# Cross attention of a hybrid block on the raw residual: transposes inside the output projection, key products by head, value products by head pair

## The chip, the cores and the metric

One core of a Trainium2 chip runs one launch that computes one layer of a hybrid encoder block, all in float32, for 512 tokens of width 1024. The metric is the device time of the launch in microseconds. Five compute engines are named as in the profile: PE (matmuls and transposes), ACT (copies, squares, exponentials), DVE (vector work that reads PSUM or SBUF), POOL (SBUF only) and SP (it issues most DMAs). Each runs its own instructions in order.

## The reference, cut to what matters

```python
h = rmsnorm(x, g_mix);  x = x + parallel_mixers(h, ...)        # ends in merged @ w_out
h = rmsnorm(x, g_x);    m = rmsnorm(mem, g_mem)                 # x: 512 x 1024, mem: 256 x 1024
q = (h @ w_cq)          # 512 x (4 heads x 128)
k = (m @ w_ck);  v = (m @ w_cv)                                 # 256 x (4 x 128)
p = softmax(q k^T * 128 ** -0.5, axis=-1)                       # per head, 512 x 256
x = x + (p v) @ w_co
h = rmsnorm(x, g_ffn);  x = x + hierarchical_moe(h, ...)        # 4 groups, top 1; 8 experts in it, top 2
out = rmsnorm(x, g_final)
rmsnorm(x, g) = x * rsqrt(mean(x * x) + 1e-6) * g
```

Since the root of a token is one factor for its whole row, q and the scores of a token can carry it or leave it out until the softmax. The 32 experts have 3 MB of weights each (gate and up 1024 x 256, down 256 x 1024).

## The kernel before

`job_order()` writes one list of jobs for PE, by hand; every other engine walks the same list in the same order and does its part of each job. A job is a tuple. Its product goes to one of eight PSUM banks, given out in turn (`bank_index`, L295 to L312); a job waits until the job that had the bank before it is emptied (`before_in_bank`), by ACT or by DVE (`emptied_by`), unless that one is in `PARTIAL`, whose sums are left standing for a later job. `emptied` counts jobs in the order of the list, so a job of DVE counts as emptied only when DVE has finished all that stands ahead of it. `wo` jobs sit in the bank of their `wp`.

The residual `xres` is four tiles of 128 tokens (t = 0 to 3). Products that need more than one pass of fp32r are split: `h_hi` and `w_high` are rounded copies (ACT), `h_lo` and `w_low` the remainders (DVE, POOL), and `split_sums` adds hi*hi, hi*lo and lo*hi (L1032 to L1034), so one 128 x 512 product over K of 128 is three matmuls. Weights come through a ring of three 1 MB chunks. ACT makes the high part of a chunk (`high_part`) and POOL its low part (`low_part`, L839), at the job named in `split_at`; SP loads the next chunk when the low part is made, or for unsplit weights when their last job is done.

The jobs around the change, in order:

- `wp`, `wo` (n, t): the two halves of K of the output projection, columns 512 n, tile t, 12 matmuls each. DVE adds the sum to `xres` (L1949).
- `hT x` (t, q): four PE transposes of tile t, half q of its columns, into one bank; DVE scales by the norm's gains into `hT` (L1794), ACT makes `h_hi` (`high_of_hT`), DVE `h_lo` of the first half (`low_of_hT`, L1748) and POOL of the second (L845). Before them, ACT squares each row (L1603), DVE takes the roots for two tiles at a time (`rms`), and ACT scales the rows (`scaled_rows`, L1472) into two buffers.
- `ck` (hp): the keys of a pair of heads from `memT`; `cq` (h): the queries of head h, 24 matmuls; ACT copies them to `cqT`.
- `xs` (t, hp): scores of tile t and head pair hp. DVE takes the negated maximum (L1972), ACT the exponentials and their sums (L1621), DVE the reciprocals (L1976), POOL scales the probabilities (L904).
- `xp` (t, hp): four transposes of the probabilities; ACT copies them to `probT[t % 2]`.
- `xv` (t): the value product of all four heads, a bank each tile. ACT makes its high part in `h_hi`, DVE its low part (L1959), which empties it.
- `co` (t, n): the projection of the heads, 12 matmuls; DVE adds it to `xres` (L1980), ACT squares (L1640).
- `hT ffn`, `rt`, `pos` (t): transposes for the router, router logits, slots. In `rt` DVE runs a chain of some fifteen small operations (L1989 to L1758). `ra`, `g0`, `ls`, `most` end the list.

SP's queue, in its own order: chunks; expert 0's weights behind the first cq chunk, when `merged_ready` is full; expert 1's when the last ck is done; parts of 3 when cq(3) is done; expert 5's (in the ring) when the last chunk's low part is made; one part of 2 after the last `xs`, one after xv(3), the last and one of 3 after co(3,1); expert 4's after the last normed row; then each expert's buffer is refilled as soon as the expert six before it has left it (L792, L794).

## Time and profile before

| what | us |
|---|---|
| median of 3 runs | 861.79 (860.40 to 869.06) |
| profiled execution, its own time | 860.8 |
| its span | 859.0 |
| PE busy | 787.2 (92%) |
| DVE, ACT, POOL busy | 358.4, 242.3, 289.3 |
| DMA, mean over the span | 189 GB/s |

The span is the profiled part of one execution; the execution's own time is 1.8 us longer. Busy shares are means over stages: PE is busy nearly throughout, the DMA engines are full only in the last third, where the experts' weights come in.

### The profile page before, as it was taken

To read this page: it belongs to the slowest core of one execution; us is meant where nothing else is said; L and a number is where in the kernel's file an instruction comes from. 1 tells how busy PE (TensorE), PEld (TensorE's weight loads), DVE (VectorE), ACT (ScalarE), POOL (GpSimd) and SP (SyncE) were. 2 spreads that over 40 slices of the span, in tenths; PEclk is the share of its full clock that TensorE was granted. 3 is DMA by queue.
4 is the path that set the end of the run, shared out by engine and by line. 5 is a ranking of instruction groups with operands and counts; after the bars stand their busy time and mean duration, and the time that the engine had idled before them with its cause. 6 is when DMAs were issued, how large, how long until landed. Compare 5 with 4: busy or idle time off the path is not lost. (4 is left out here: it accounts for less than half of the span.)

```text
span 859.0 us, 14860 instructions
## 1 busy us (share of the span) xinstructions
PE 787.2 (92%) x5803; PEld 639.6 (74%) x5803; DVE 358.4 (42%) x757; ACT 242.3 (28%) x421; POOL 289.3 (34%) x255
## 2 busy tenths in 40 slices
PE   5999999899899999999999898998999999887884
PEld 4888888788788877788887777886777777665651
DVE  6479752473574683336612712363222222211115
ACT  4332342112212559422214444331111111100102
POOL 3824434442242244043350634233333333322110
PEclk9999999999999999999999899999999999999997
DMA  9754423402202250455476273659999999999946
GB/s 258 144 103 91 103 45 66 83 1 50 50 1 50 50 142 11 94 142 153 98 146 196 54 241 116 252 219 343 391 389 388 388 383 390 384 383 391 390 157 243
DMA packets 73230, 162.77 MB, mean 189 GB/s; under 512 B 18834, under 2 KB 46306, under 8 KB 65240
## 3 DMA queue, kind: packets, MB, share of 16 engines
q1 hardware_dynamic: 65712, 150.66, 55.6%
q0 software_dynamic: 5472, 9.82, 3.4%
q10 hardware_dynamic: 1992, 1.55, 0.9%
q8 instruction: 36, 0.59, 0.3%
q14 instruction: 18, 0.15, 0.1%
HBM read 157.31 MB, written 13.04 MB: 198 GB/s over the span
## 5 line engine op out<-in xcount | busy, mean ns | idle before, releaser
L1032 PE MATMUL bank<-h_hi,w_high 128*128 128x512 f32 x296 | 122.4, 414 | 2.3 <-DVEq L560 2.0
L839 POOL TENSOR_TENSOR ring_low<-ring,w_high 128x2048 fp32r<-128x2048 f32 (+1 forms) x16 | 71.3, 4459 | 135.1 <-ACT w_high L1448 118.4
L1033 PE MATMUL bank<-h_lo,w_high 128*128 128x512 f32 x296 | 115.8, 391 | 0.0
L1373 PEld LDWEIGHTS bank<-arena,hT 128*64 128x64 f32 x1728 | 96.8, 136 | 24.9 <-issue 24.5
L1373 PE MATMUL bank<-arena,hT 128*64 128x128 f32 x1728 | 100.6, 274 | 8.8 <-DMA arena<-in_w_exp_up 7.9
L839 POOL TENSOR_TENSOR w_low<-ring,w_high 128x2048 fp32r<-128x2048 f32 x14 | 64.4, 4598 | 81.7 <-ACT w_high L1448 81.6
L2043 DVE SCALAR_TENSOR_TENSOR rt<-rt,bank 128x128 f32<-128x128 f32 x32 | 9.2, 288 | 176.9 <-ACT rt L1664 176.9
L1448 ACT ACTIVATE w_high<-ring 128x2048 fp32r<-128x2048 f32 (+1 forms) x32 | 58.8, 1838 | 47.1 <-PE bank L1034 30.9
L1032 PEld LDWEIGHTS bank<-h_hi,w_high 128*128 128x128 f32 x296 | 55.8, 188 | 14.8 <-DVEq L560 2.3
L1034 PE MATMUL bank<-h_hi,ring_low 128*128 128x512 f32 x168 | 66.1, 394 | 0.0
L1033 PEld LDWEIGHTS bank<-h_lo,w_high 128*128 128x128 f32 x296 | 55.8, 188 | 9.5
L1383 PE MATMUL bank<-arena,rt 128*64 128x512 f32 x216 | 52.3, 605 | 10.4 <-DVE rt L2047 10.4
L956 POOL DMA_INDIRECT y_half<-rows,cst x32 | 32.6, 1019 | 79.4 <-ACT rows L1668 78.6
L1032 PE MATMUL bank<-w_high,h_hi 128*128 128x512 f32 (+1 forms) x144 | 51.7, 359 | 1.5 <-ACT w_high L1448 1.5
L1034 PE MATMUL bank<-w_high,h_lo 128*128 128x512 f32 (+1 forms) x144 | 51.0, 354 | 0.0
L1034 PE MATMUL bank<-h_hi,w_low 128*128 128x512 f32 x128 | 50.0, 390 | 0.0
L1668 ACT ACTIVATE rows<-bank 128x512 f32<-128x512 f32 x32 | 19.1, 598 | 109.3 <-PE bank L1383 109.3
L1033 PE MATMUL bank<-w_low,h_hi 128*128 128x512 f32 (+1 forms) x128 | 44.7, 349 | 0.0
L1664 ACT ACTIVATE rt<-bank 128x128 f32<-128x128 f32 x32 | 8.9, 278 | 109.2 <-PE bank L1373 109.2
L951 POOL DMA_INDIRECT hT<-h_rows,rt x31 | 30.4, 981 | 24.5 <-POOL rt L946 23.8
L1448 ACT ACTIVATE arena<-bank 128x512 f32<-128x512 f32 (+1 forms) x39 | 23.3, 597 | 53.7 <-PE bank L1034 35.6
L1034 PEld LDWEIGHTS bank<-h_hi,ring_low 128*128 128x128 f32 x168 | 31.5, 188 | 7.4
(309 smaller groups left out, 1412.0 us busy)
## 6 DMA issues: line engine op xcount, KB each, us to landing
arena<-in_w_exp_gate SPq DMA_DIRECT2D x27, 1024.0 KB
arena<-in_w_exp_up SPq DMA_DIRECT2D x27, 1024.0 KB
arena<-in_w_exp_down SPq DMA_DIRECT2D x27, 1024.0 KB
ring<-in_w_in SPq DMA_DIRECT2D x33, 512.0 KB, 6.7
ring<-in_w_exp_gate SPq DMA_DIRECT2D x5, 1024.0 KB
ring<-in_w_exp_up SPq DMA_DIRECT2D x5, 1024.0 KB
ring<-in_w_exp_down SPq DMA_DIRECT2D x5, 1024.0 KB
xres<-in_x SPq DMA_DIRECT2D x8, 512.0 KB, 7.0
```

Source lines behind the costliest of these rows:

```text
L839: after(pool.tensor_tensor(low, full, high, ALU.subtract), w_lo)
L951: pool.indirect_dma_start(out=xg[:, b % DEEP, :], out_offset=None, in_=h_rows, in_offset=bass.IndirectOffsetOnAxis(ap=idx[b][0:CAP, :], ax ...
L956: pool.indirect_dma_start(out=y_half, out_offset=bass.IndirectOffsetOnAxis(ap=at_y, axis=0), in_=ysb[:, y, :], in_offset=None, bounds_chec ...
L1032: pe.matmul(o, l_hi, r_hi, start=(n == 0), stop=False)
L1033: pe.matmul(o, l_hi, r_lo, start=False, stop=False)
L1034: ins = pe.matmul(o, l_lo, r_hi, start=False, stop=(n == count - 1))
L1373: ins = pe.matmul(bank[CAP * half:CAP * half + CAP, 1, P * n:P * n + P], xgT[:, x, kk, :], w[:, kk, P * half:P * half + P], start=(kk == 0 ...
L1383: ins = pe.matmul(bank[CAP * half:CAP * half + CAP, o, :], hidT[:, CAP * kk:CAP * kk + CAP], down[:, kk, 512 * half:512 * half + 512], sta ...
L1448: after(nc.scalar.activation(o, i, ACT.Copy, scale=scale), s)
L1664: nc.scalar.activation(gate_th, bank[:, 1, 0:P], ACT.Tanh, scale=0.5).then_inc(gth_ready, 1)
L1668: nc.scalar.activation(ysb[:, y, :], bank[:, 4 + b % 2, :], ACT.Copy).then_inc(y_sb, 1)
L2043: nc.vector.scalar_tensor_tensor(out=gated, in0=gate_th, scalar=1.0, in1=bank[:, 1, 0:P], op0=ALU.add, op1=ALU.mult).then_inc(step["dve"], 1)
```

## The change

The transposes for the cross attention read `xres` itself. Those of the first half of the columns (q = 0) stand among the jobs of the second half of the output projection, those of the second half behind each tile's `wo`. The queries and scores are then those of the raw residual times the gains; the root comes in as the scale of the exponential and as a factor on the maximum (one DVE operation more per `xs`). `scaled_rows` and the two-tile roots of this phase go; the squares are taken into `rows`, and one four-tile root is taken by DVE behind the last low part. `ck` is split by head, the second pair's behind cq(1). `xw` (t) is the value product of heads 0 and 1, left standing in its bank, `xv` (t) that of heads 2 and 3 in the same bank. For tiles 2 and 3 (`t >= X_POOL`) DVE makes both halves of the low part. ACT makes the high part of the last co chunk at xs(0,1) and no longer at xv(0). SP waits for `ck` (1,1) where it waited for `ck` (1), and since chunks go by first use, the first cq chunk now comes ahead of the second ck chunk. The diff, with little of what stands around it:

```diff
@@ -166,17 +166,17 @@
         jobs += [(k, f) for k in ("ub", "ua") for f in range(4 * half, 4 * half + 4)]
-    jobs += [(k, n, t) for n in range(2) for k in ("wp", "wo") for t in range(NT)]
-    turn = [[("hT", "x", t, q) for q in range(2)] for t in range(NT)]
-    jobs += turn[0] + turn[1] + [("ck", 0)] + turn[2] + turn[3] + [("ck", 1)]
-
-    for hp in range(2):
-        jobs += [("cq", 2 * hp)] + [("xp", t, 0) for t in range(2)] * hp + [("cq", 2 * hp + 1)] + [("xs", t, hp) for t in range(NT)]
-    jobs += [("xp", 0, 1), ("xp", 1, 1)]
-    tail = [("xv", 0), ("xp", 2), ("xv", 1), ("co", 0), ("xp", 3), ("xv", 2), ("T", 0), ("co", 1), ("rt", 0),
-            ("xv", 3), ("T", 1), ("co", 2), ("rt", 1), ("pos", 0), ("T", 2)]
+    jobs += [(k, 0, t) for k in ("wp", "wo") for t in range(NT)]
+    turn = [[("hT", "x", t, q) for t in range(NT)] for q in range(2)]
+    jobs += [("wp", 1, 0), ("wp", 1, 1), turn[0][0], ("wp", 1, 2), turn[0][1], ("wp", 1, 3), turn[0][2]]
+    jobs += [("wo", 1, 0), turn[0][3], ("wo", 1, 1), turn[1][0], ("wo", 1, 2), turn[1][1], ("wo", 1, 3), turn[1][2]]
+    jobs += [("ck", 0, 0), turn[1][3], ("ck", 0, 1), ("cq", 0), ("cq", 1), ("ck", 1, 0), ("ck", 1, 1)] + [("xs", t, 0) for t in range(NT)]
+    jobs += [("cq", 2), ("cq", 3), ("xp", 0, 0), ("xp", 1, 0), ("xs", 0, 1), ("xs", 1, 1), ("xs", 2, 1), ("xw", 0), ("xw", 1)]
+    jobs += [("xp", 0, 1), ("xs", 3, 1), ("xp", 1, 1), ("xp", 2, 0)]
+    jobs += [("xv", 0), ("xp", 3, 0), ("xv", 1), ("xw", 2), ("xp", 2, 1), ("co", 0, 0), ("co", 0, 1), ("xp", 3, 1)]
+    tail = [("xv", 2), ("xw", 3), ("T", 0), ("co", 1), ("rt", 0), ("xv", 3), ("T", 1), ("co", 2), ("rt", 1), ("pos", 0), ("T", 2)]
     for stage, t in tail:
-        if stage in ("xv", "rt", "pos"):
+        if stage in ("xv", "xw", "rt", "pos"):
@@ -187,7 +187,7 @@
-PARTIAL = ("gp", "wp", "g0", "ra")
+PARTIAL = ("gp", "wp", "g0", "ra", "xw")
@@ -195,6 +195,7 @@
 LAST_TILE = NT - 1
+X_POOL = 2
@@ -288,6 +289,7 @@
         split_at[said.get(c) or first_use[split_chunks[m - 1]]] = m
+    high_at = {("xs", 0, 1) if job == ("xv", 0) else job: m for job, m in split_at.items()}
@@ -299,6 +301,8 @@
             bank_index[job] = bank_index["wp", job[1], job[2]]
+        elif job[0] == "xv":
+            bank_index[job] = bank_index["xw", job[1]]
@@ -759,7 +763,7 @@
                 if n == place[("co", 0)]:
-                    job_done(sp, ("ck", 1))
+                    job_done(sp, ("ck", 1, 1))
@@ -868,7 +872,7 @@
                     after(pool.tensor_scalar(gain_b, gain_b, 0.5, None, ALU.mult))
-                if job[:2] == ("hT", "x") and c == 1:
+                if job[:2] == ("hT", "x") and c == 1 and job[2] < X_POOL:
@@ -1066,8 +1070,8 @@
                     _, phase, t, q = job
-                    if phase == "ffn":
-                        job_empty(pe, ("co", t, q))
+                    if phase in ("ffn", "x"):
+                        job_empty(pe, ("co", t, q) if phase == "ffn" else ("wo", q, t))
@@ -1076,11 +1080,9 @@
                         return ins
-                    else:
-                        pe.wait_ge(rows_ready, NORM_TILES[phase] - NT + t + 1)
+                    pe.wait_ge(rows_ready, t + 1)
                     for j in range(4):
-                        source = mem_rows[:, t] if phase == "mem" else rows[:, t % 2]
-                        ins = pe.transpose(oh4[:, j], source[:, (4 * q + j) * P:(4 * q + j + 1) * P], ident)
+                        ins = pe.transpose(oh4[:, j], mem_rows[:, t, (4 * q + j) * P:(4 * q + j + 1) * P], ident)
@@ -1253,9 +1255,8 @@
                     job_empty(pe, ("hT", "mem", NM - 1, 1))
-                    for i in range(2):
-                        ins = sums(o[:, MEM * i:MEM * i + MEM], [(wide(chunks_of(job)[0])[:, kk, P * i:P * i + P], memT[:, kk, :]) for kk in range(KD)])
-                    return ins
+                    i = job[2]
+                    return sums(o[:, 0:MEM], [(wide(c0)[:, kk, P * i:P * i + P], memT[:, kk, :]) for kk in range(KD)])
@@ -1264,13 +1265,13 @@
                     pe.wait_ge(h_hi_ready["x"], 2 * NT)
-                    pe.wait_ge(h_lo_ready["x"], NT)
-                    pe.wait_ge(pool_lo_ready["x"], NT)
+                    pe.wait_ge(h_lo_ready["x"], 2 * NT - X_POOL)
+                    pe.wait_ge(pool_lo_ready["x"], X_POOL)
                     job_empty(pe, ("cq", 2 * hp + 1))
-                    job_empty(pe, ("ck", hp))
+                    job_empty(pe, ("ck", hp, 1))
@@ -1282,10 +1283,10 @@
                     return ins
-                if k == "xv":
-                    t = job[1]
-                    job_empty(pe, ("xp", t, 1))
-                    for h in range(X_HEADS):
+                if k in ("xw", "xv"):
+                    t, hp = job[1], int(k == "xv")
+                    job_empty(pe, ("xp", t, hp))
+                    for h in (2 * hp, 2 * hp + 1):
@@ -1458,18 +1459,11 @@
+                if phase == "x":
+                    job_done(act, ("wo", 1, t))
                     copy(h_hi[:, 4 * q:4 * q + 4, t * P:(t + 1) * P], hT[:, 4 * q:4 * q + 4, t * P:(t + 1) * P], h_hi_ready[phase])
-
-            def scaled_rows(phase, t, source):
-
-                base = NORM_TILES[phase]
-                act.wait_ge(rstd_ready, {"mem": 1, "x": 2 + t // 2}[phase])
-                if t >= 2:
-                    job_done(act, ("hT", phase, t - 2, 1))
-                dst = rows[:, t % 2, :] if phase != "mem" else source
-                after(nc.scalar.activation(dst, source, ACT.Copy, scale=rstd[:, base + t:base + t + 1]), rows_ready)
@@ -1489,16 +1483,23 @@
                     return
+                act.wait_ge(rstd_ready, 1)
                 for t in range(tiles):
-                    scaled_rows(phase, t, source(t))
+                    after(nc.scalar.activation(source(t), source(t), ACT.Copy, scale=rstd[:, base + t:base + t + 1]), rows_ready)
+
+            def x_square(t):
+
+                n = NORM_TILES["x"] + t
+                job_empty(act, ("wo", 1, t))
+                after(nc.scalar.activation(rows[:, t % 2, :], xres[:, t, :], ACT.Square, accum_out=squares[:, n:n + 1]), squared)
                 c = job[-1]
-                if job in split_at:
-                    high_part(split_at[job])
+                if job in high_at:
+                    high_part(high_at[job])
@@ -1596,34 +1597,29 @@
                 if k == "wo" and job[1] == 1:
-                    base = NORM_TILES["x"]
-                    if c == 2:
-                        scaled_rows("x", 0, xres[:, 0, :])
-                    job_empty(act, job)
-                    after(nc.scalar.activation(x_row[c], xres[:, c, :], ACT.Square, accum_out=squares[:, base + c:base + c + 1]), squared)
-                    if c == 2:
-                        scaled_rows("x", 1, xres[:, 1, :])
-                    for t in (2, 3) if c == 3 else ():
-                        scaled_rows("x", t, xres[:, t, :])
-                        high_of_hT("x", t - 2)
-                    for t in (2, 3) if c == 3 else ():
-                        high_of_hT("x", t)
+                    if c < 2:
+                        x_square(c)
+                if job[:2] == ("hT", "x") and c == 1:
+                    high_of_hT("x", job[2])
+                    for t in (2, 3) if job[2] == NT - 1 else ():
+                        x_square(t)
                     if t == 0 and hp == 0:
-                        act.wait_ge(h_lo_ready["x"], NT)
-                        act.wait_ge(pool_lo_ready["x"], NT)
+                        act.wait_ge(h_lo_ready["x"], 2 * NT - X_POOL)
+                        act.wait_ge(pool_lo_ready["x"], X_POOL)
                         h, so = 2 * hp + i, 16 * t
+                        n = NORM_TILES["x"] + t
                         ins = nc.scalar.activation(prob[t][:, h, :], o[:, MEM * i:MEM * i + MEM], ACT.Exp, bias=xstat[:, so + 4 + h:so + 5 + h],
-                                                   accum_out=xstat[:, so + 8 + h:so + 9 + h])
+                                                   scale=rstd[:, n:n + 1], accum_out=xstat[:, so + 8 + h:so + 9 + h])
                 if k == "xp":
-                    if job[1] >= 2 and c == 0:
-                        job_done(act, ("xv", job[1] - 2))
+                    if job[1] >= 2:
+                        job_done(act, ("xv" if c else "xw", job[1] - 2))
@@ -1746,6 +1742,10 @@
                 after(tt(h_lo[s], hT[s], h_hi[s].bitcast(F32), ALU.subtract), h_lo_ready[phase])
+                if phase == "x" and t >= X_POOL:
+                    dve.wait_ge(h_hi_ready[phase], 2 * t + 2)
+                    s = (slice(0, P), slice(4, KD), slice(t * P, (t + 1) * P))
+                    after(tt(h_lo[s], hT[s], h_hi[s].bitcast(F32), ALU.subtract), h_lo_ready[phase])
@@ -1778,8 +1778,6 @@
                         mark(ins) if h < 3 else after(ins, y_ready)
-                if job == ("wo", 1, 2):
-                    rms(NORM_TILES["x"], 2, rstd_ready)
@@ -1797,6 +1795,8 @@
                             low_of_hT(phase, t)
+                            if phase == "x":
+                                rms(NORM_TILES["x"], NT)
@@ -1947,8 +1947,6 @@
                     after(stt(out=xs, in0=o, scalar=0.5, in1=xs, op0=ALU.mult, op1=ALU.add), e)
-                    if (n, t) == (1, 3):
-                        rms(NORM_TILES["x"] + 2, 2, rstd_ready)
@@ -1960,7 +1958,7 @@
                 if k == "ck":
-                    after(nc.vector.tensor_copy(ckT[:, 2 * c:2 * c + 2, :], o.rearrange("p (h m) -> p h m", h=2)), e)
+                    after(nc.vector.tensor_copy(ckT[:, 2 * job[1] + c, :], o[:, 0:MEM]), e)
@@ -1969,7 +1967,9 @@
                     job_done(dve, job)
-                    after(nc.vector.tensor_reduce(xstat[:, 16 * t + 4 + 2 * hp:16 * t + 6 + 2 * hp], o.rearrange("p (h m) -> p h m", h=2), AX, ALU.max, negate=True), xmax_ready)
+                    least, n = xstat[:, 16 * t + 4 + 2 * hp:16 * t + 6 + 2 * hp], NORM_TILES["x"] + t
+                    after(nc.vector.tensor_reduce(least, o.rearrange("p (h m) -> p h m", h=2), AX, ALU.max, negate=True))
+                    after(ts(least, least, rstd[:, n:n + 1], None, ALU.mult), xmax_ready)
```

## Rows read from the trace of the kernel before

**Rows 1.** The page: span; TensorE's granted clock and the DMA share in 40 slices.
```profile
span 859.0 us, 14860 instructions
...
PEclk9999999999999999999999899999999999999997
...
DMA  9754423402202250455476273659999999999946
```

**Rows 2.** Chain that ended last, in order of time: start us, us, what.
```profile
624.59 17.37 DMA ring<-in_w_exp_up
```

**Rows 3.** Windows: length, busy of PE, PEld, DVE, ACT, POOL; granted clock, DMA share, GB/s.
```profile
558.00:568.00 10.00, 10.00 (x69) 9.09 (x69) 7.21 (x35) 5.97 (x9) 3.70 (x11) 1.00 0.13 54
...
573.00:583.00 10.00, 9.71 (x118) 9.45 (x118) 5.89 (x29) 0.92 (x1) 2.14 (x8) 1.00 1.00 400
```

**Rows 4.** Timeline of SP's DMA queue, expert weights: start us, us, what.
```profile
568.81 0.38 SPq L727 DMA_DIRECT2D arena<-in_w_exp_down  x1
...
585.89 0.36 SPq L792 DMA_DIRECT2D arena<-in_w_exp_gate  x1
```

**Rows 5.** Windows around the two falls of TensorE's clock, columns as in Rows 3.
```profile
466.00:470.00 4.00, 2.26 (x18) 1.95 (x18) 0.69 (x1) 3.90 (x5) 0.00 (x0) 1.00 0.07 27
...
477.00:484.00 7.00, 4.41 (x18) 3.98 (x19) 6.62 (x12) 5.13 (x7) 2.44 (x2) 0.64 0.71 153
...
522.00:526.00 4.00, 2.35 (x15) 1.67 (x13) 2.31 (x6) 3.77 (x15) 2.43 (x3) 1.00 0.88 365
...
526.00:532.00 6.00, 5.06 (x33) 4.85 (x32) 0.67 (x2) 4.74 (x7) 3.93 (x3) 0.72 0.00 0
```

**Rows 6.** Timeline of PE: start us, us, line, what, count, idle before and its releaser.
```profile
465.75 0.39 PE L1034 MATMUL bank<-w_high,h_lo 128*128 128x512 f32 x1
...
469.84 7.07 PE L1025 MATMUL bank<-arena,ring 128*128 128x256 f32 x32
...
479.01 1.92 PE L1083 MATMUL bank<-cst,rows 128*128 128x128 f32 x8 [2.09 <-ACT rows L1472]
...
483.24 8.37 PE L1025 MATMUL bank<-arena,ring 128*128 128x256 f32 x32
...
503.33 3.69 PE L1025 MATMUL bank<-arena 128*128 128x256 f32 x16 [0.79 <-issue]
...
527.21 3.46 PE L1025 MATMUL bank<-rows,arena 128*128 128x128 f32 x16 [0.94 <-ACT rows L1448]
```

**Rows 7.** Timelines of POOL (L839, L845) and DVE (L1717, L1748), columns as in Rows 6.
```profile
470.91 4.53 POOL L839 TENSOR_TENSOR w_low<-ring,w_high 128x2048 fp32r<-128x2048 f32 x1 [19.74 <-ACT w_high L1448]
...
480.33 1.27 POOL L845 TENSOR_TENSOR h_lo<-hT,h_hi 128x512 fp32r<-128x512 f32 x1 [4.89 <-ACT h_hi L1448]
...
472.03 3.43 DVE L1717 TENSOR_SCALAR tiny<-tiny 128x2 f32<-128x2 f32 x1 [5.09 <-ACT hT L1603]
...
480.56 1.58 DVE L1748 TENSOR_TENSOR h_lo<-hT,h_hi 128x512 fp32r<-128x512 f32 x1
```

**Rows 8.** Timelines of ACT and POOL in the second half of the cross attention.
```profile
521.69 0.47 ACT L1621 ACTIVATE hT<-bank,tiny 128x256 f32<-128x256 f32 x1 [2.11 <-PE bank L1025]
...
527.73 1.91 ACT L1448 ACTIVATE w_high<-ring 128x2048 fp32r<-128x2048 f32 x1
...
523.26 1.04 POOL L904 TENSOR_TENSOR hT<-hT,tiny 128x512 f32<-128x512 f32 x1 [6.39 <-DVE tiny L1976]
```

**Rows 9.** Timelines of PE (first three) and DVE about the first router tile.
```profile
549.34 2.03 PE L1025 MATMUL bank<-rows,arena 128*128 128x128 f32 x16
...
551.21 1.04 PE L1072 MATMUL bank<-cst,xres 128*128 128x128 f32 x8
...
552.00 0.48 PE L1032 MATMUL bank<-w_high,h_hi 128*128 128x512 f32 x1
...
549.65 0.22 DVE L1989 SCALAR_TENSOR_TENSOR rt<-bank,tiny,rt 128x4 f32<-128x4 f32 x1 [0.90 <-PE bank L1025]
...
553.04 0.69 DVE L1959 TENSOR_TENSOR h_lo<-bank,h_hi 128x512 fp32r<-128x512 f32 x1
```

## Prediction, on record before the changed kernel was run

> **What bounds the kernel now.** Read the page's slices first [rows 1]: from about 580 us on the DMA engines are full to the end, and the chain [rows 2] turns from PE to expert weights at 624.6 us and stays with them until 806. So the expert stage is a stream of fixed length, and only its start can move. What sets the start is in the windows and SP's queue: at 558 to 568 us the DMA engines are nearly empty (0.13), from 573 us they are full [rows 3]; the loads that fill them are issued when co(3,1) is done (568.8) and, from expert 6 on, when expert 0's gate and up products are done (585.9) [rows 4]. Both hang on PE. A microsecond that PE gains before them moves the whole stream, and the end, by one. So the question is when PE reaches the router; the experts and the tail only shift.
>
> Between the end of the output projection (the last of its matmuls starts at 465.75, 0.23 behind the one ahead, so it ends at 466.0 [rows 6]) and the router PE loses time in two ways. It idles: 1.7 us in 466 to 470 [rows 5], 2.09 and then 0.58 us before the transposes of tiles 2 and 3, 0.79 before the first scores [rows 6], 1.65 in 522 to 526 [rows 5], 0.94 before xv(0) [rows 6]. And its clock falls twice to the 1.2 GHz level, after the idle of 2.09 and after the idles of 522 to 527 (granted 0.64 and 0.72 in those windows [rows 5]). The first fall costs 3.1 us: eight transposes take 1.92 for 1.04 [rows 6, 9], twice, and ck(1) 8.37 for ck(0)'s 7.07 [rows 6]. The second costs 1.6: xv(0) takes 3.46 [rows 6], xv(3) 1.87 (549.34 to the next group, 551.21 [rows 9]).
>
> **The change, part by part.** I lay the new order out with durations of the rows: an output-projection job is 12 matmuls of 0.227, 2.72 us; four transposes 0.4 (0.79 for eight, 551.21 to 552.00 [rows 9]; I take 0.43, with the switch of bank); one head's key product half of 7.07, 3.54; a cq job 24 matmuls, 5.44; xs 0.86 (3.46 for four [rows 6]); an xw or xv, half of the old xv, 0.9. The number of matmuls stays.
>
> *To cq(0).* The old second half of the projection begins 8 x 2.72 ahead of 466.0, at 444.2. The new order puts 32 transposes and two key products with it: 21.8 + 8 x 0.43 + 7.1 = 32.3, so PE could begin cq(0) at 476.5. The two row scalings per pair of tiles, the rstd chain and PE's waits on them are gone: nothing waits for the norm before the exponentials (the four-tile root follows at 480 to 482 on DVE, 15 us before scores; cost nothing, hidden by cq and ck). The old cq(0) began after all of ck, at 491.3 (483.24 and 8.37, less the overlap [rows 6]); with the later two key products set off it would be 484.2. So the order is worth 7.7 here.
>
> *But the low parts are late.* ACT makes the high part of the cq weights after hi(1), at 467.9 to 469.8 (1.91 as in [rows 8]), and POOL then takes 4.53 for the low one [rows 7], 469.9 to 474.5. DVE comes to low(1), a subtraction of two SBUF operands, at 470.3. Such DVE work does not run beside POOL's: the 128x2 operation at 472.03 took 3.43 and ended with POOL's at 475.4, and a low part at 480.56 took 1.58, 0.7 behind POOL's end at 481.6 [rows 7]. So low(1) ends at 475.2, ck(0,0)'s copy and hT(3,1) at 476.3, and then come four subtractions of 0.72, since tiles 2 and 3 now have both halves on DVE: 479.2. cq(0) waits for the last: idle 2.8. Gain so far 7.7 - 2.8 = 4.9. The 0.4 us by which POOL is ahead of DVE decide this order; the other one is rival (e).
>
> *Scores.* ck(1,0) and ck(1,1) stand behind cq(1) and cover its copy: the 0.79 idle [rows 6], and 0.4 of overlap behind it, go. cq(3)'s copy is covered by xp(0,0) and xp(1,0), another 1.0. By xs(0,1) the gain is 7.1: 512.5 for 519.7. DVE's extra scaling of the maxima has no row; a small operation takes about 0.2 alone, and up to a whole product of POOL's (1.04 [rows 8]) if it blocks as the one at 472.03 did. I find it 0.4 late at three of eight, laid beside POOL's queue; in the first half that is behind cq(2) and costs nothing. ACT's exponentials take their scale from a column now: now 0.47 each [rows 8]; I take no more, and 0.1 on each would still stay behind PE's work in the first half.
>
> *xp to co(0,0).* ACT now does the high part of the last co chunk (1.91 [rows 8]) ahead of the exponentials of xs(0,1). Its queue: copies of cq(3), xp(0,0), xp(1,0) until 513.7, high part until 515.6, two pairs until 518.0; POOL's product follows one reciprocal later, 517.2 to 518.3 (1.04). PE is through xw(1) at 516.9: it waits 1.4 for xp(0,1), then 0.25 for xp(1,1), 0.7 for the copy behind xv(1), 0.3 and 0.8 for xv(0) and xv(1) to leave the banks that xp(2,1) and co(0,0) take. Those 3.5 stand against about 4.8 of old idling and slow clock there: gain 8.4 at co(0,0), equal work against equal work.
>
> *Two new bank waits.* The turn of banks shifts. co(1,0) comes into the bank of xv(2), and is behind ACT's square, xp(3,1)'s copy, xv(2)'s high part and DVE's low one: 1.3 of idle; 7.1 is left. co(2,0) comes into the bank of xv(3), which it did not before. DVE empties xv(3) only after the router chain of rt(0): 549.65 to 553.04, plus 0.69 [rows 9], so 4.4 behind the end of rt(0). PE needs only xv(3) at 0.9 and eight transposes, 1.8, before co(2,0). Idle 2.7. What is left at co(2,0) is 4.4 (547.6 for 552.0). From there PE runs as before. The same addition over the old order falls 0.3 short of its trace, so I take 4.1.
>
> *SP.* cq(0)'s chunk loads before expert 0's weights, cq(2)'s at 476.8, landing near 483, before ACT's use; the last co chunk lands behind 3 MB of expert 1 near 511.6, 2 us before ACT wants it. Costs nothing; if it came 1 us after 513.7, that microsecond would be PE's.
>
> *Clock.* The old order lost 4.7 to it, of which part lay in idles that it shortened; that is in the 4.1. The new one has two idles of 2.7 to 2.8, longer than the 2.09 behind the first fall [rows 6]; but 1.7 in 466 to 470 brought none [rows 5]. A fall with busy work behind costs what the second did, 1.6. None costs 0; both long ones (3.1 each) 6.2. I take one of 1.6: 4.1 - 1.6 = 2.5.
>
> **Sum.** 2.5 us off the profiled execution's 860.8 (span 859.0 and 1.8 around it) is 858.3. The median of the runs shown, 861.79, stands 1.0 above that execution, so a median would be **859.3**.
>
> **Rivals.** (a) *The clock never falls:* 4.1 gained, 857.7. For it: full-rate work for 30 us ahead of the stall. Against: 2.09 sufficed [rows 5, 6]. (b) *The new waits are not there:* DVE slips between POOL's, and the router chain is shorter than I read; then 4.1 + 2.8 + 2.7 = 9.6, 852.2. For it: only their absence removes the ground for both falls too. Against: both waits are in the order of the code, with rows for each length. (c) *Slower, the clock at cq(0) and co(2,0):* it falls at both idles and stays down through the next waits, as the first fall did; 2 x 3.1 = 6.2 against 4.1, so 863.9. It decides once more than 4.1 us is lost, that is 8 us at 1.2 GHz. Against: behind both stalls stand 10.9 and 5.4 us of matmuls without a wait, where the old fall had more waits. (d) *The start doesn't carry:* the stream begins when it did, 861.8. Against: the DMA engines are at 0.13 before it [rows 3]. (e) *DVE's low(1) gets in ahead of POOL:* POOL then runs 471.0 to 475.6, DVE does hT(3,1) under it, the four subtractions end at 478.5, the idle before cq(0) is 2.0 and the sum 0.8 larger, 858.5. For it: 0.4 us is little beside ACT's and POOL's own start times; against, the order as the rows' durations give it. The Trainium skill, "SBUF — State Buffer", section "Who interferes with whom", has a rule for this: of a GpSimd operation and a VectorE one with two SBUF inputs, the one that is issued first keeps the shared ports for the whole instruction and the other blocks.
>
> **Chances.** Forecast (one fall, or two short ones, 858.5 to 861) 0.36; (e) 0.14; (a) 0.17; (b) 0.15; (c) 0.13; (d) 0.05. The range 852.5 to 863.5 leaves out the faster part of (b) and most of (c). What can be told from no change here is 1%, 8.6 us: faster than 853.2 needs the larger part of (b), 0.11; slower than 870.4 has 0.02; within 0.87.
>
> **What would show it.** In the changed trace: no idle on PE among transposes and projection; DVE's L1748 for tile 1 stretched to the end of POOL's L839, PE idle 2 to 2.8 before cq(0); idle 2.7 before co(2,0), released by DVE's L1959 behind the router chain; granted clock under 1.0 near either. Expert 0 then starts 2 to 4 us ahead of 582. If the DMA engines show a gap in 590 to 800 us, or PE is still idle for other reasons before rt(0), the reading is wrong.

## The result, and the profile after

The changed kernel was **slower**: median 868.06 us (865.78 to 872.34, 17 runs) against 863.4 (860.3 to 871.55, 17 runs) for the kernel before in the same comparison; ratio 1.0061 [1.0039, 1.0082]. The profiled execution took 870.23 (span 868.4, mean granted clock 0.974). The loss of 0.6% is under the 1% that the forecast called no change, but outside its range of 852.5 to 863.5: all 17 runs of the changed kernel took 865.78 or more, 12 of the 17 of the kernel before less. The comparisons leave out runs over 1.5% above the fastest of the same kernel (none here, some further below), which is one reason why a ratio is not the quotient of the two medians beside it.

The page of the changed kernel, to be laid beside [rows 1]. From about 600 us on the stream of experts fills the DMA engines as it did; new are a 7 in the granted clock ahead of it, and a 5 in the DMA share where [rows 1] has its first 9 of that stretch.

```profile
span 868.4 us, 14852 instructions
...
PEclk9999999999999999999999999978999999999997
...
DMA  9755513302202261364494474275999999999946
```

Two rows of untouched code settle where the comparison starts. This is the same group of matmuls, first in the timeline of PE of the kernel before, then of the changed one: start, duration, line, count, idle before.

```profile
363.60 6.71 PE L1025 MATMUL bank<-ring,arena 128*128 128x256 f32 x30 [1.81 <-DVE arena L1794]
```

```profile
365.55 4.77 PE L1029 MATMUL bank<-ring,arena 128*128 128x256 f32 x21 [1.81 <-DVE arena L1792]
```

The changed kernel is 1.95 us late some 80 us before the first instruction that the change moves. Its granted clock was 0.91 in 160 to 180 us, 1.00 in the profiled execution of before; between 167 and 230 us 1.6 of the 1.95 is lost, 0.3 was there before. These instructions are the same in both kernels, so it comes off every number that follows. Below, "the mark" is the start of this group.

Windows of the changed kernel, columns as in Rows 3:

```profile
466.00:477.00 11.00, 11.00 (x57) 9.36 (x57) 7.99 (x7) 6.99 (x10) 7.12 (x3) 1.00 0.00 1
477.00:484.00 7.00, 4.21 (x15) 3.20 (x14) 6.13 (x19) 2.93 (x5) 0.00 (x0) 0.83 0.57 121
484.00:491.00 7.00, 7.00 (x30) 5.74 (x29) 0.43 (x2) 2.52 (x2) 2.55 (x1) 0.92 0.89 182
522.00:532.00 10.00, 7.97 (x54) 6.76 (x55) 3.18 (x8) 7.08 (x17) 7.43 (x5) 1.00 0.04 17
548.00:558.00 10.00, 7.56 (x34) 6.20 (x34) 4.21 (x17) 3.22 (x6) 3.42 (x11) 0.83 0.42 160
573.00:583.00 10.00, 10.00 (x52) 10.00 (x52) 4.56 (x25) 1.15 (x1) 3.11 (x11) 0.54 0.98 376
583.00:600.00 17.00, 15.46 (x137) 13.77 (x136) 5.32 (x25) 0.70 (x3) 3.82 (x7) 0.67 0.44 159
588.00:594.00 6.00, 6.00 (x63) 5.75 (x64) 2.88 (x14) 0.42 (x2) 1.07 (x3) 0.50 0.02 7
```

The first window answers to the idles and the waits of 466 to 470 in [rows 5]: PE is now busy without a gap. The next two hold the wait before cq(0) and a fall of the clock behind it. The fifth holds the same at co(2,0). The sixth and seventh are the surprise: PE is full and the clock is at or near the 1.2 GHz level (0.54, then 0.67) where [rows 3] has 1.00. The last one lies within the seventh: the clock is at 0.50, and the DMA engines stand still (0.02), where the same window of the kernel before has them full (1.02).

Timeline of PE of the changed kernel: cq(0), xp(0,1), xv(1), co(0,0), co(1,0), co(2,0).

```profile
481.62 0.74 PE L1036 MATMUL bank<-h_hi,w_high 128*128 128x512 f32 x1 [2.79 <-DVE h_lo L1748]
...
522.50 0.63 PE L1284 MATMUL bank<-cst,hT 128*128 128x128 f32 x4 [1.46 <-POOL hT L908]
...
527.19 2.05 PE L1029 MATMUL bank<-rows,arena 128*128 128x128 f32 x16 [0.90 <-ACT rows L1449]
...
530.54 0.50 PE L1036 MATMUL bank<-w_high,h_hi 128*128 128x512 f32 x1 [0.61 <-DVE h_lo L1957]
...
540.50 0.50 PE L1036 MATMUL bank<-w_high,h_hi 128*128 128x512 f32 x1 [1.08 <-DVE h_lo L1957]
...
552.23 0.50 PE L1036 MATMUL bank<-w_high,h_hi 128*128 128x512 f32 x1 [2.44 <-DVE h_lo L1957]
```

These six are waits of the forecast (2.8, 1.4, 0.7, 0.8, 1.3, 2.7), each behind the engine that it named; the two small ones that it also had, 0.25 before xp(1,1) and 0.3 before xp(2,1), did not come. The old gaps of [rows 6] are gone.

Timelines of DVE and of POOL behind the first of them: the low part of tile 1 on DVE, then the low part of the cq weights on POOL.

```profile
472.60 4.68 DVE L1744 TENSOR_TENSOR h_lo<-hT,h_hi 128x512 fp32r<-128x512 f32 x1
...
480.67 0.69 DVE L1748 TENSOR_TENSOR h_lo<-hT,h_hi 128x512 fp32r<-128x512 f32 x1
```

```profile
472.20 4.53 POOL L843 TENSOR_TENSOR w_low<-ring,w_high 128x2048 fp32r<-128x2048 f32 x1 [0.69 <-ACT w_high L1449]
```

POOL is 0.4 ahead, and a subtraction that takes 0.69 alone takes 4.68. It ends 0.55 behind POOL's end at 476.73.

The last stretch before the experts, first the kernel before, then the changed one (timeline of PE; the 32 matmuls of L1337, L1338 are the first of the job g0, the x64 or x37 of L1373, L1374 are the start of expert 0).

```profile
571.04 0.60 PE L1025 MATMUL bank<-rt,cst 128*128 128x32 f32 x4 [0.63 <-issue]
571.48 1.06 PE L1302 MATMUL bank<-rt,hT 128*128 128x36 f32 x8
572.37 3.76 PE L1337 MATMUL bank<-rows,hT 128*128 128x64 f32 x32
...
581.96 2.29 PE L1373 MATMUL bank<-arena,hT 128*64 128x128 f32 x37
```

```profile
572.81 0.60 PE L1029 MATMUL bank<-rt,cst 128*128 128x32 f32 x4 [0.62 <-issue]
573.25 1.40 PE L1303 MATMUL bank<-rt,hT 128*128 128x36 f32 x8
574.45 7.07 PE L1338 MATMUL bank<-rows,hT 128*128 128x64 f32 x32
...
591.54 5.09 PE L1374 MATMUL bank<-arena,hT 128*64 128x128 f32 x64
```

From the start of g0 to expert 0 it was 9.59 us and is 17.09: **7.5 us lost at the 1.2 GHz level**, in the same instructions, with the same idle of 0.62 ahead of them. From the start of expert 0 to the end it is 277.0 us before (859.0 - 581.96) and 276.9 after. Inside, it is not the same: expert 0's first 64 matmuls take 5.09 for 3.77, so SP's loads behind them (585.89 in [rows 4]) and the turn of the chain to the expert weights (624.59 in [rows 2]) both come 10.9 us later, and some 1.5 us of that is made up before the end; how is not shown. The load in SP's queue, and the turn of the chain:

```profile
596.80 0.36 SPq L796 DMA_DIRECT2D arena<-in_w_exp_gate  x1
```

```profile
635.50 16.41 DMA ring<-in_w_exp_up
```

The account of the two spans (868.4 - 859.0 = 9.4), by marks on PE. Late start: +1.95. At co(2,0): 552.23 for 552.00 [rows 9], so 1.7 gained. Between there and g0 (574.45 for 572.37) 1.85 given back, 1.5 of it the clock behind co(2,0): about seven matmuls from 553.6 to 556.6 stand 0.43 apart for 0.227. Then the 7.5. Sum 9.6; the 0.2 over the 9.4 is made up behind expert 0.

### The profile page after: what moved, and what is told of

It reads as the page before. It is cut to its first block, busy times and chain, and to the rows that moved or that the text cites. A ratio compares the mean times of both kernels' runs of the same rounds, so it can differ in the third digit from the quotient of the medians.

```text
span 868.4 us, 14852 instructions
## 1 busy us (share of the span) xinstructions
PE 796.9 (92%) x5803; PEld 648.5 (75%) x5803; DVE 361.0 (42%) x757; ACT 239.2 (28%) x417; POOL 286.1 (33%) x253
## 4 chain that ended last, share of the span: by engine, by line
PE 58%; DMA 22%; DVE 10%; issue 4%; ACT 4%; POOL 2%; SPq 1%; DVEq 0%; POOLq 0%; ACTq 0%
PE bank L1029 13%; DMA arena<-in_w_exp_up 12%; PE bank L1036 12%; PE bank L1038 11%; PE bank L1037 11%; DMA ring<-in_w_exp_up 8%; PE bank L1374 4%; PE bank L1384 2%; PE bank L1338 2%; ACT xres L1566 1%; DVE arena L1779 1%; DVE h_lo L1744 1%; PE bank L1361 1%; DMA arena<-y_half 1%; PE bank L1237 1%
## 5 line engine op out<-in xcount | busy, mean ns | idle before, releaser
L1374 PEld LDWEIGHTS bank<-arena,hT 128*64 128x64 f32 x1728 | 98.1, 138 | 24.3 <-issue 24.0
L1374 PE MATMUL bank<-arena,hT 128*64 128x128 f32 x1728 | 101.9, 276 | 8.2 <-DMA arena<-in_w_exp_up 7.3
L1384 PEld LDWEIGHTS bank<-arena,rt 128*64 128x64 f32 x216 | 13.1, 136 | 30.9 <-DVE rt L2047 15.5
```

The costliest lines, as they stand in the source:

```text
L1374: ins = pe.matmul(bank[CAP * half:CAP * half + CAP, 1, P * n:P * n + P], xgT[:, x, kk, :], w[:, kk, P * half:P * half + P], start=(kk == 0 ...
L1384: ins = pe.matmul(bank[CAP * half:CAP * half + CAP, o, :], hidT[:, CAP * kk:CAP * kk + CAP], down[:, kk, 512 * half:512 * half + 512], sta ...
```

## The experiments

Theory A: the order and the waits are worth what was laid out, about 1 us in sum with two short falls of the clock, and the loss is the slow stretch at g0. Theory B: the loss is the waits themselves. Theory C: the difference is a matter of which execution was profiled. All ratios are to the kernel before in the same comparison, whose medians were 864.95 (35 runs, e1 to e4, on one chip), 865.2 (23 runs, e5 to e8) and 862.5 (22 runs, e9 to e12, both on another).

**e1_before_again: the kernel before, with no edit.**

> The kernel before, unchanged, for the spread of its own runs and a second trace. Theory A (the clock in the stretch of the last router tile and g0 is a matter of how the jobs fall in time, and the profiled run of before was one of the lucky ones): the times lie in two groups some 8 us apart, 860 to 864 and 866 to 872, and time goes with the mean granted clock of the run, about 8 to 9 us per 0.01. Theory B (the changed kernel is slower because of its new waits alone): no such relation, and every trace of before has full clock from 550 to 600 us.

Measured: median 862.14 (855.49 to 871.65, 12 runs), ratio 0.9931 [0.9888, 0.9973]. It is the same kernel, so the ratio should be 1, and the interval leaves 1 out: the intervals of this document are narrower than what the same kernel does when it is timed again, and a ratio within 0.7% of 1 shows little by itself. The 1.0061 of the result is of that size; what speaks for it is that the two sets of runs hardly overlap. The runs of e1 scatter: 8 of the 12 took 855.5 to 863.9 with a mean clock of 0.978 to 0.990, 4 took 867.4 to 871.7 with 0.971 to 0.974. Over all 80 runs of the kernel before in the three comparisons the expected two groups are not apart: the times go from 855.8 to 872.5 with no gap over 1.7. Its profiled execution (span 865.7) shows the g0 stretch in the unchanged kernel; two of its windows and its g0:

```profile
560.00:574.00 14.00, 13.19 (x84) 11.86 (x84) 10.88 (x54) 7.13 (x13) 6.23 (x20) 0.93 0.44 162
574.00:583.00 9.00, 9.00 (x45) 9.00 (x44) 3.94 (x22) 0.40 (x1) 1.34 (x5) 0.50 1.00 399
```

```profile
573.57 7.07 PE L1337 MATMUL bank<-rows,hT 128*128 128x64 f32 x32
```

The slow g0 is not made by the change. The kernel before has it in a part of its runs; the changed one had a mean clock of 0.971 to 0.981 in all 17, its fastest run 865.78. C holds for a part: the profiled execution of before was one that was spared.

**e2_early_high: the high part of the cq weights is made two jobs earlier.**

```
-    said = {..., ("cq", 0): ("wo", 1, 3), ...}
+    said = {..., ("cq", 0): ("wo", 1, 1), ...}
```

> The changed kernel with the high and low parts of the first cq chunk two jobs earlier, at wo(1,1) for wo(1,3), so that POOL's low part is over before DVE's low(1). My reading of the lock: DVE's low(1) takes 0.7 for 4.68, the idle before cq(0) falls from 2.79 to under 0.6, and the fall of the clock behind it (1.5) goes too: 2.3 us at cq(0) by idle alone, up to 3.8. Rival (the four subtractions on DVE alone make cq(0) late): idle stays over 2. In the total: 2 to 4 us less if the clock in the g0 stretch stays as it is, some 8 more or less if that moves.

Measured: 864.03 (855.78 to 866.24, 12 runs), ratio 0.9945 [0.9909, 0.9981]. Timeline of PE at cq(0), and the window about it:

```profile
479.42 0.47 PE L1036 MATMUL bank<-h_hi,w_high 128*128 128x512 f32 x1 [0.53 <-DVE h_lo L1748]
```

```profile
477.00:491.00 14.00, 13.47 (x60) 11.02 (x59) 4.49 (x16) 5.18 (x7) 1.68 (x1) 1.00 0.71 152
```

POOL's subtraction moved ahead of DVE's low parts; low(1) takes 1.17 for 4.68 (0.7 was expected). The idle falls from 2.79 to 0.53, and the fall of the clock behind it is gone with it. co(2,0), with its idle of 2.44 as it was, starts at 548.39 for 552.23, so 3.8 earlier: 2.26 of idle and 1.5 of clock. Both executions are equally late at the mark of 365 us. The g0 stretch stays (32 matmuls in 7.07 us). Two runs of the 12 took 855.78 and 857.28 with clocks of 0.992 and 0.988, as high as those of kernels without the slow stretch (e4, e10); they have no trace, but likely escaped it.

**e3_xv3_ahead: xv(3) stands ahead of the first router tile.**

```
-    tail = [..., ("co", 1), ("rt", 0), ("xv", 3), ("T", 1), ("co", 2), ...]
+    tail = [..., ("co", 1), ("xv", 3), ("rt", 0), ("T", 1), ("co", 2), ...]
```

> The changed kernel with xv(3) ahead of rt(0) in the list, so that DVE empties xv(3) before its router chain. Theory (bank wait behind the router chain): the idle of 2.44 before co(2,0) falls to about 0.3 and the clock fall behind it (1.5) goes, 2 to 4 us less at co(2,0). Rival (co(2,0) waits for something else, such as xv(2)'s low part or the weights): the idle stays. In the total, beside the g0 stretch as above.

Measured: 864.53 (860.03 to 868.14, 12 runs), ratio 1.0019 [0.9984, 1.0054]. A window of it, and PE at cq(0):

```profile
540.00:560.00 20.00, 19.91 (x116) 17.35 (x117) 8.94 (x35) 8.03 (x12) 4.99 (x18) 1.00 0.41 161
```

```profile
481.42 0.76 PE L1036 MATMUL bank<-h_hi,w_high 128*128 128x512 f32 x1 [2.79 <-DVE h_lo L1748]
```

DVE now empties xv(3) before the router chain, not behind it. The idle of 2.44 and the fall behind it are gone, that before cq(0) stays. g0 begins at 569.68 for 574.45, 4.5 earlier when counted from the mark, and still takes 7.07. The total doesn't show this gain against the kernel before (1.0019).

**e4_warm: three matmuls of no use on 128x512 operands before the position products of the last tile; their result is read by nobody.**

```
+                    if t == 2:
+                        job_empty(pe, ("pos", 1))
+                        for _ in range(3):
+                            pe.matmul(bank[:, 5, :], ident, cst[:, 0:512], start=True, stop=True)
```

> The changed kernel with three 128x512 float32 matmuls of no use (into a free bank) ahead of pos(2), 2.6 us of PE work of which 0.6 fills an idle. Theory A (the clock falls at 573.8 us because PE has only small matmuls around the last router tile, and stays down through g0, at a price of 7 to 8 us): the clock stays at the 2.4 GHz level from 570 to 595 us, g0's 32 matmuls take 3.6 and not 7.07, and the total is 5 to 6 us less (7.5 won, 2.0 paid). Theory B (the clock there is not what costs): 2 us more.

Measured: 861.4 (858.01 to 862.58, 12 runs), ratio 0.9927 [0.9895, 0.996], all clocks 0.985 to 0.993. Granted clock 1.00 throughout 560 to 600, span 860.0. PE about the old slow stretch:

```profile
574.25 3.77 PE L1342 MATMUL bank<-rows,hT 128*128 128x64 f32 x32
```

B falls: the two waits are untouched (idles of 2.79 and 2.44 are still there), and the time is 6.7 below the changed kernel's median, though in another comparison (the kernel before had 863.4 there and 864.95 here). A's part on g0 holds.

**e5_before_warm: the same three matmuls in the kernel before.**

> The kernel before with the same three matmuls of no use ahead of pos(2). If the g0 stretch at the 1.2 GHz level is a loss that both kernels can take (the second trace of before had it, the first had not), the upper group of before (866 to 872) goes: all runs lie in 858 to 865, median 861 to 863, and the spread is as small as that of the changed kernel with them (858.0 to 862.6). If only the changed kernel is prone to it, before pays 2 us for nothing and keeps its two groups.

Measured: 862.49 (858.05 to 865.19, 12 runs), ratio 0.9995 [0.9963, 1.0027]. The ratio shows no gain, but the scatter is smaller: 7 of the 23 runs of before took 866 or more, none of these 12. Beside e4 (861.4) no price of the change can be read: the medians differ by 1.1 us, the ratios (0.9927 and 0.9995) by 0.7%, some 6 us, and the two ran on different chips.

**e6_both: the edits of e2 and e3 together, without added matmuls.**

> The changed kernel with both order edits (high part of cq at wo(1,1), xv(3) ahead of rt(0)). Theory: both idles (2.79 and 2.44) are gone, each with the fall behind it, so co(2,0) starts 5 to 8 us ahead of the changed kernel's; the g0 stretch stays a matter of chance, so the runs lie between 853 and 864 with a median near 861. Rival (idle taken away only moves to the next wait): co(2,0) gains less than 3 us.

Measured: 859.45 (856.61 to 863.07, 12 runs), ratio 0.9942 [0.9911, 0.9973]. All 12 clocks lie at 0.977 to 0.984, and the profiled execution shows why (window, then g0):

```profile
560.00:574.00 14.00, 13.38 (x75) 13.17 (x74) 6.39 (x35) 2.25 (x4) 3.63 (x12) 0.62 0.98 373
```

```profile
562.43 6.16 PE L1338 MATMUL bank<-rows,hT 128*128 128x64 f32 x32
```

Counted from the mark, co(2,0) starts 6.3 earlier than in the changed kernel (5 to 8 were expected). With both long waits out of the way the clock still falls at g0. So the slow g0 is not an after-effect of the waits.

**e7_both_warm3: e6 with three matmuls.**

> Both order edits and the three matmuls of no use. Theory: the three effects add, as they lie in different stretches: the changed kernel with the three matmuls alone had 861.4, less 4.7 to 5.2 of idle and up to 3 of clock: 854 to 857, all runs within 5 us. If they do not add (the clock falls elsewhere instead): 858 or more.

Measured: 854.95 (853.82 to 857.5, 6 runs), ratio 0.9891 [0.984, 0.9942]. That is within what was expected (854 to 857), so the three effects add.

**e8_both_warm1: e6 with one matmul.**

> The same with one matmul of no use for three, 0.85 us of which 0.6 fills an idle. If one is enough to keep the clock up: 1.5 us less than with three, 853 to 856. If it is not: some runs are 7 us longer than the rest and the median is above that with three.

Measured: 852.44 (851.93 to 855.3, 6 runs), ratio 0.9861 [0.981, 0.9912]. Its PE in the stretch (the matmul of no use counts as two records), and the window:

```profile
564.22 1.02 PE L1321 MATMUL bank<-cst 128*128 128x512 f32 x2
565.08 0.53 PE L1029 MATMUL bank<-rt,cst 128*128 128x32 f32 x4
...
566.34 3.76 PE L1342 MATMUL bank<-rows,hT 128*128 128x64 f32 x32
...
575.92 3.76 PE L1378 MATMUL bank<-arena,hT 128*64 128x128 f32 x64
```

```profile
560.00:574.00 14.00, 13.58 (x104) 12.36 (x102) 9.40 (x49) 4.33 (x8) 4.41 (x14) 1.00 0.89 339
```

One matmul of 0.86 us (564.22 to 565.08), put where PE idled 0.62, keeps the clock up: g0 to expert 0 takes 9.58 again. Beside e6, which differs by this matmul alone and ran in the same comparison, the median is 7.0 lower (852.44 for 859.45) and no run of one is as long as the shortest of the other. This is the cleanest price of the slow stretch in run times.

**e9_before_warm1: the kernel before with one matmul.**

> The kernel before with one matmul of no use ahead of pos(2): the base for what the change is worth once the g0 stretch is out of play. If one matmul keeps the clock up there: 1.5 us less than with three (862.5), 861, no run over 865. If not: the upper group (866 to 872) is back.

Measured: 860.13 (856.99 to 865.45, 12 runs), ratio 0.9991 [0.9956, 1.0026]; 8 of the 22 runs of before took 866 or more, none of these. Its profile answers a question that the forecast had closed too early. PE and two windows:

```profile
468.93 1.58 PE L1083 MATMUL bank<-cst,rows 128*128 128x128 f32 x8 [1.30 <-ACT rows L1475]
470.30 8.27 PE L1025 MATMUL bank<-arena,ring 128*128 128x256 f32 x32
478.98 1.07 PE L1083 MATMUL bank<-cst,rows 128*128 128x128 f32 x8 [0.41 <-ACT rows L1475]
...
482.39 7.07 PE L1025 MATMUL bank<-arena,ring 128*128 128x256 f32 x32
```

```profile
470.00:477.00 7.00, 7.00 (x29) 6.03 (x28) 4.71 (x9) 1.88 (x3) 4.52 (x1) 0.81 0.00 0
...
526.00:532.00 6.00, 6.00 (x45) 5.57 (x44) 1.38 (x2) 3.85 (x5) 4.37 (x1) 1.00 0.00 0
```

The instructions of [rows 6], with the same idle of 1.30 at the same time: there it brought no fall (ck(0) 7.07, ck(1) 8.37), here it did (8.27). PE then came later to the next transposes, where an idle of 0.41 is left of 2.09, and ck(1) was spared (7.07); the fall of 526 to 532 [rows 5] is not there either. So an idle does not decide alone, and the falls of [rows 5] are those of one execution. The trace of e5 shows the same as that of e9.

**e10_after_warm1: the changed kernel with one matmul.**

> The changed kernel with one matmul of no use ahead of pos(2). My step of the prediction, that the changed order itself gains 4.1 us less what its two idles cost in clock (1.5 each): 1 to 3 us under the kernel before with the same matmul, on the same chip. Theory B (the change is slower by its order): 4 to 5 us over it, as the plain kernels were (868.06 and 863.4).

Measured: 859.27 (median of 12 with one far outlier, below; the others 855.24 to 861.24), ratio 0.9955 [0.9922, 0.9987]. Both long idles are there, and both falls; PE, then two windows:

```profile
548.55 0.50 PE L1036 MATMUL bank<-w_high,h_hi 128*128 128x512 f32 x1 [2.44 <-DVE h_lo L1961]
```

```profile
477.00:484.00 7.00, 6.08 (x20) 4.90 (x21) 3.07 (x14) 2.16 (x3) 0.00 (x0) 0.76 1.07 228
...
551.00:560.00 9.00, 9.00 (x50) 7.76 (x50) 3.25 (x13) 3.12 (x5) 1.52 (x6) 0.88 0.12 50
```

Beside e9, in one comparison, the median is 0.9 us lower (859.27 for 860.13; 1 to 3 were expected). The two ratios, 0.9955 and 0.9991, each have an interval of 0.3% to either side, so the sign of the change isn't shown by the times. The traces don't show it either, as the table behind e12 says.

**e11_pool_lows: e8 with the low parts of all four tiles on POOL (X_POOL 4 for 2).**

> Both order edits, one matmul of no use, and X_POOL 4 for 2: POOL makes the second half of the low part of tiles 2 and 3 too, as before the change. If the halves on DVE are what the change needs them for (POOL's 1.27 beside DVE's 0.7, and the two do not run together): the idle before cq(0) is 1 to 2 for 0.53, and the time 0.5 to 1.5 us over the next kernel. Rival (with the early high part it no longer matters): within 0.3 us.

Measured: 851.61 (849.15 to 853.03, 6 runs), ratio 0.9862 [0.9807, 0.9917]. It was expected to be 0.5 to 1.5 slower than e12, and is 2.4 faster. PE comes to cq(0) without a wait; the timeline of PE, then of POOL:

```profile
474.99 3.62 PE L1029 MATMUL bank<-arena,ring 128*128 128x256 f32 x16
478.70 0.47 PE L1036 MATMUL bank<-h_hi,w_high 128*128 128x512 f32 x1
```

```profile
476.84 1.72 POOL L849 TENSOR_TENSOR h_lo<-hT,h_hi 128x512 fp32r<-128x512 f32 x1 [2.16 <-ACT h_hi L1453]
```

POOL's last low part ends at 478.56, just ahead of PE. With the weights done early, POOL has the time; moving these subtractions to DVE was not needed.

**e12_best_again: e8 once more, in the comparison of e11.**

> Both order edits and one matmul of no use once more, beside the three others on one chip: 852 to 853, 7 to 8 us under the changed kernel with the matmul alone (2.3 and 2.2 of idle, the falls behind both, 1.5 each).

Measured: 853.98 (851.64 to 855.41, 6 runs), ratio 0.9893 [0.9838, 0.9948]. That is 5.3 under e10, where 7 to 8 were expected. e11 is 2.4 below it, with overlapping runs; counted from the mark its g0 starts only 0.5 earlier. e8, e11 and e12 are 8.5 to 12.8 us under the kernel before by the medians, 1.1 to 1.4% by the ratios.

**The traces side by side.** These are times from the mark (363 us in the kernel before) to the start of co(2,0) and of g0, from the timelines of PE. They leave out what differs ahead of the mark and what g0 itself costs. Matmuls of no use lie between the two points.

| order | trace | to co(2,0) | to g0 |
|---|---|---|---|
| before | before | 188.4 | 208.8 |
| before | e1 | 189.1 | 210.2 |
| before | e5, three matmuls | 185.0 | 207.1 |
| before | e9, one matmul | 185.0 | 205.4 |
| changed | after | 186.7 | 208.9 |
| changed | e4, three matmuls | 186.7 | 210.3 |
| changed | e10, one matmul | 186.7 | 208.6 |
| changed, one order edit | e2; e3 | 182.8; 184.0 | 204.9; 204.4 |
| changed, both order edits | e6; e8; e12 | 180.4; 180.4; 180.4 | 200.7; 200.7; 200.7 |
| both edits, low parts on POOL | e11 | 179.9 | 200.2 |

The changed order took the same time to co(2,0) in its three traces, with both falls in each. The order before took 3.4 to 4.1 us less in two of its traces than in the other two, by its own falls. So at co(2,0) the change is 1.7 to 2.4 us ahead of two traces of before and 1.7 behind the other two, and at g0, with one matmul in both kernels, it is 3.2 behind (e10 and e9). Its sign is open. With both order edits it is 4.7 ahead (e8 and e9).

## Why the prediction was wrong

**The bound: right.** What PE loses before expert 0 comes out at the end (277.0 and 276.9 from expert 0 on). It is not one to one to the tenth: over all 14 traces that stretch takes 275.0 to 277.6. Rival (d) is out. The forecast took a gap of the DMA engines in 590 to 800 us as a sign against its reading, and there is one, in 588 to 594 us (share 0.02). It bears the reading out: the stream stood because PE had not come to expert 0.

**To cq(0), and the low parts: right.** Idle 2.79 for 2.8, released by the last of the four subtractions. With the late start taken off, cq(0) begins at 479.7 where the text had 479.3. POOL was first, so rival (e) did not come. For the shared ports the rule that it cites from the Trainium skill, "SBUF — State Buffer", section "Who interferes with whom", holds: POOL's was issued first and DVE's, with two inputs in SBUF, stood until its end (4.68 us for 0.69). The text read DVE's end as 0.7 behind POOL's; [rows 7] give 0.54 (482.14 for 481.60), and here it is 0.55.

**Scores, xp to co(0,0), the two bank waits: right.** 1.46, 0.90, 0.61, 1.08 and 2.44 us for 1.4, 0.7, 0.8, 1.3 and 2.7; two more of 0.25 and 0.3 did not come. Rival (b), that they are not there, is out. e2 and e3 took one each away by what the text named as its cause, and only that one went.

**The sum at co(2,0): 0.9 too high.** 4.1 was forecast, 2.6 with the one fall of 1.5 that lies ahead of it; 1.7 was measured. 0.4 is there at cq(0), 0.5 in the work between.

**The clock: this step failed.** "A fall with busy work behind costs what the second did, 1.6 ... I take one of 1.6": the price was right (1.5 each), the count was not. Both long idles brought one: in the changed kernel, and again in e10. The second fall is 1.5 of the miss. Rival (c) had both places, but at 3.1 each. The other side of the sum has the same fault: "The old order lost 4.7 to it" is true of one execution. In e5 and e9 the same order lost 3.4 us less on the way to co(2,0), twice what the changed order gained there (1.7).

**"From there PE runs as before": the sentence that broke the forecast.** This step failed too, and it is the larger miss. It took the granted clock of 1.00 from 573 us on [rows 3] as a property of the code. It was a property of that execution. e1 shows the same code at 0.50. The stretch from g0 to expert 0 takes 17.09 for 9.59, so it costs 7.5 us when it is slow (7.0 in run times, e6 and e8), and it was slow in the profiled execution of the changed kernel; the clocks of its 17 runs, all under those of e4 and e10 (but for the outlier of e10), make the same likely for the others. No part of the forecast, and no rival, had this term, and it is as large as all that the new order was to gain up to cq(0), 7.7.

**The base.** The text put the median 1.0 above the profiled execution, from three runs. Over 17 runs it is 2.6 above (863.4 for 860.8).

Against the profiled execution, 858.3 was forecast and 870.23 came: 11.9 apart, made of 7.5 (g0), 1.95 (late start), 1.5 (the second fall), 0.9 (the sum), and 0.1 of rest.

**What stays open.** Whether the change by itself gains or loses. And why the changed kernel is hit at g0 in, as it seems, all of its runs, and the one before only in a part. How large a part is not known either: 31 of its 80 runs took over 866, but 46 had a mean clock of 0.981 or less, the highest of the changed kernel's 17. The instructions of the stretch are the same and so is the idle in it. e9 shows that whether a given idle brings a fall differs between executions of the same instructions. The Trainium skill, "TensorE: Matmul & The Clock Gate", section "What's actually happening", says that the clock's monitor runs freely and isn't reset when a kernel starts. That would fit e9, but no run here tests it or separates it from a cause in the order. e6 rules out the long waits as the cause; beyond that nothing is shown.

## What to carry to other kernels

A granted clock of 1.00 in one profile is a fact of that execution: where a stretch has only small matmuls (36 to 64 columns here), price it at both clock levels, and look at the clocks and times of all runs for two groups before taking an execution as the base. When a small reordering is to be judged, first take the stretch that flips out of play (one matmul did it), in both kernels, and then compare several traces of each from a common mark: here the kernel before still differed from itself by 3.4 to 4.1 us. A wait that an order creates is read off a profile well (the six that came within 0.3 us, two small ones of eight not there), and the cheapest cure is the one at its cause: an earlier high part and one swapped job were worth 5.3 us by the medians (e12 for e10) and 7.9 at g0 by the traces, while for the whole change not even the sign is shown.

## What the hardware showed that was not expected

- PE was busy in every microsecond of 573 to 583 by the records, and the granted clock was 0.54 there. It stayed at the 1.2 GHz level for some 20 us, to about 594, in which PE was without idle on small matmuls and then on the first products of expert 0.
- One matmul of 128x512, 0.86 us, ahead of that stretch kept the clock at 1.00 (e8 to e12), as three did (e4, e5, e7). Of the 72 runs of these eight (seven kernels, since e8 and e12 are one) one alone took over 866; of the 80 runs of the kernel before in the same three comparisons 31 did.
- That one, of e10, took 1317.35 us at a mean clock of 0.555: nearly the whole run at 1.2 GHz. It was seen once.
- Code that no edit touched moved by up to 3.8 us between executions: the mark of 363.60 stood at 361.83 in e10 and at 365.64 in e8. All that stand over 365 had a clock of 0.91 in 160 to 180 us. e1 had that too and stood at 363.41, as it had been 1.8 us ahead of the kernel before at 165 us.
